# One matmul on nine partitions for the bias table of a decoder layer, spread to 128 rows by its store to DRAM

## What is computed

```python
def t5_bucket(dist):
    n = jnp.maximum(dist, 0)
...
    return jnp.where(n < max_exact, n, large)
...
    def head_bias(bucket):
        nq, nk = bucket.shape
        return rel_bias[bucket].reshape(nq, nk, G, HPG).transpose(2, 3, 0, 1)
...
        s_w = jnp.einsum('bqghd,bkgd->bghqk', qi, kw) * scale + head_bias(t5_bucket(dist))
```

## Time and profile before

| what | us |
|---|---|
| median of three runs | 2054.9 |
| lowest and highest | 2054.63, 2056.81 |
| span of the profiled execution | 2052.7 |
| PE busy in the span | 2019.7 |
| DVE busy | 1393.5 |
| ACT busy | 876.4 |

### The profile page before, as it was taken

The page is one execution under the profiler, slowest core; times in us unless marked ns, Lnnn a source line. Parts: engine busy times, 40 slices in busy tenths (PEclk is TensorE's granted clock), DMA queues, the critical chain, the costliest instruction groups (busy, mean ns, idle before and its releaser), DMA issues.

```text
span 2052.7 us, 26825 instructions
## 1 busy us (share of the span) xinstructions
PE 2019.7 (98%) x9299; PEld 1602.7 (78%) x9299; DVE 1393.5 (68%) x1852; ACT 876.4 (43%) x1127; POOL 36.6 (2%) x56
## 2 busy tenths in 40 slices
PE   7999999999999999999999999999999999999998
PEld 4668888788888888787787878788888888888886
DVE  3557878877778888996556669777774455445454
ACT  4334344344443333543445644544444444434343
POOL 0000000000000000000005000000000000000000
PEclk8999999999999999999999999999999999999999
DMA  9988988899899889798966148599986677676654
GB/s 359 386 314 308 355 318 297 282 299 279 275 320 327 309 308 343 234 367 282 295 195 240 42 147 303 165 281 291 294 249 195 193 206 203 194 217 199 199 185 134
DMA packets 341269, 533.10 MB, mean 260 GB/s; under 512 B 80825, under 2 KB 95252, under 8 KB 340280
## 3 DMA queue, kind: packets, MB, share of 16 engines
q1 hardware_dynamic: 340280, 527.81, 77.8%
q10 hardware_dynamic: 896, 4.06, 0.5%
HBM read 520.04 MB, written 3.89 MB: 255 GB/s over the span
## 4 chain that ended last, share of the span: by engine, by line
PE 94%; DVE 2%; issue 1%; ACT 1%; DMA 1%; ACTq 0%; SPq 0%
PE ps L810 29%; PE ps L812 29%; PE ps L811 29%; PE ps L854 2%; PE ps L839 1%; PE ps L872 1%; DVE ada_acc L1903 1%; PE ps L1333 1%; PE ps L1336 1%; PE ps L1363 1%; DVE w_lo L1885 1%; PE ps L1168 0%; PE ps L1058 0%; ACT w_hi L1457 0%; DMA raw<-in_w_uq_dram 0%
## 5 line engine op out<-in xcount | busy, mean ns | idle before, releaser
L1457 ACT ACTIVATE w_hi<-raw 128x1024 fp32r<-128x1024 f32 (+1 forms) x657 | 689.1, 1054 | 931.5 <-PE ps L812 554.7
L1885 DVE TENSOR_TENSOR w_lo<-raw,w_hi 128x1024 fp32r<-128x1024 f32 (+1 forms) x657 | 796.4, 1220 | 402.4 <-ACT w_hi L1457 398.3
L810 PE MATMUL ps<-w_hi,hT_hi 128*128 128x512 f32 (+1 forms) x1856 | 742.0, 400 | 7.2 <-DVE hT_lo L2020 4.3
L812 PE MATMUL ps<-w_hi,hT_lo 128*128 128x512 f32 (+1 forms) x1856 | 732.1, 394 | 0.0
L811 PE MATMUL ps<-w_lo,hT_hi 128*128 128x512 f32 (+1 forms) x1856 | 732.0, 394 | 0.0
L810 PEld LDWEIGHTS ps<-w_hi,hT_hi 128*128 128x128 f32 x1856 | 350.0, 189 | 102.1 <-issue 14.2
L812 PEld LDWEIGHTS ps<-w_hi,hT_lo 128*128 128x128 f32 x1856 | 350.1, 189 | 83.8
L811 PEld LDWEIGHTS ps<-w_lo,hT_hi 128*128 128x128 f32 x1856 | 350.4, 189 | 80.0 <-issue 0.5
L1903 DVE SCALAR_TENSOR_TENSOR ada_acc<-ada_raw,silu_c,ada_acc 128x512 f32<-128x512 f32 x420 | 315.6, 751 | 8.1
L810 PE MATMUL ps<-w_hi,actT_hi 128*128 128x512 f32 x704 | 280.0, 398 | 0.0
L812 PE MATMUL ps<-w_hi,actT_lo 128*128 128x512 f32 x704 | 279.1, 396 | 0.0
(11 more groups left out here) (235 smaller groups left out, 929.7 us busy)
## 6 DMA issues: line engine op xcount, KB each, us to landing
ada_raw<-in_w_ada_dram SPq DMA_DIRECT2D x224, 512.0 KB, 5.6
raw<-in_w_gate_dram SPq DMA_DIRECT2D x176, 512.0 KB, 4.8
raw<-in_w_up_dram SPq DMA_DIRECT2D x176, 512.0 KB, 5.0
raw<-in_w_down_dram SPq DMA_DIRECT2D x176, 512.0 KB, 4.8
raw<-in_w_in_dram SPq DMA_DIRECT2D x72, 512.0 KB, 5.8
ada_half<-in_w_ada_dram SPq DMA_DIRECT2D x16, 2048.0 KB, 12.7
raw<-in_w_out_dram SPq DMA_DIRECT2D x32, 512.0 KB, 5.0
actT_lo<-norm_tmp SPq DMA_DIRECT2D x240, 32.0 KB, 3.2
```

Source lines behind the costliest of these rows:

```text
L810: pe.matmul(bank, lhs_hi, rhs_hi, start=start, stop=False)
L812: return pe.matmul(bank, lhs_lo, rhs_hi, start=False, stop=stop)
L1457: act.activation(part(U, w_hi, s), part(U, raw, s), ACT.Copy).then_inc(hi_done, 1)
L1885: dve.tensor_tensor(part(U, w_lo, s), part(U, raw, s), part(U, w_hi, s).bitcast(F32), ALU.subtract)\
```

## The change

`rel_rep`, its copy on POOL and eight of the nine matmuls go. One matmul with the nine columns of `rel_sb` gives nine partitions of 384 numbers, one ACT copy takes them to `rev_b` (now 9 x 384), and the store writes every row 128 times: its source repeats each partition's row with a step of zero, its destination is the same DRAM tensor in another order of its dimensions. Two unused tensors keep all other addresses. The waits on `rev_done` shrink to one, ahead of panel 1 of unit 0, because the product sits in PSUM bank 3, which that panel writes.

```diff
-            pool.wait_ge(rel_landed, 16)
-            pool.wait_ge(rel_set, 2)
-            pool.tensor_copy(rel_rep[:, :, :], rel_sb[:, :].unsqueeze(2).broadcast_to([BUCKETS + 1, HEADS + 1, P]))\
-                .then_inc(rel_rep_set, 1)
...
-                if i == 2:
-                    pe.wait_ge(rev_done, HEADS + 1)
...
-                if j < 2 and u == 0:
-                    pe.wait_ge(rev_done, (6, 8)[j])
-                elif j < 2:
+                if (u, j) == (0, 1):
+                    pe.wait_ge(rev_done, 1)
+                elif u == 1 and j < 2:
                     pe.wait_ge(spilled, 2 * j + 2)
...
-            def bias_rows(first, last):
-
-                for h in range(first, last):
-                    if 4 <= h < HEADS:
-                        pe.wait_ge(rev_done, h - 3)
-                    pe.matmul(ps[:, bias_bank(h), 0:384], rel_rep[:, h, :], bucket_sb[:, :], start=True, stop=True)\
-                        .then_inc(rev_mm, 1)
+            def bias_rows():
+
+                pe.wait_ge(rel_set, 2)
+                pe.wait_ge(rel_landed, 16)
+                pe.matmul(ps[0:HEADS + 1, 3, 0:384], rel_sb[:, :], bucket_sb[:, :], start=True, stop=True)\
+                    .then_inc(rev_mm, 1)
...
-            copy_bias_rows(0, 4)
             act.wait_ge(x_landed, 16)
...
-            copy_bias_rows(4, 6)
             copy_rstd("ffn1", T_BANK)
-            copy_bias_rows(6, 8)
             first_hi(0)
             start_hi(0, 1)
-            copy_bias_rows(8, HEADS + 1)
+            act.wait_ge(rev_mm, 1)
+            act.activation(rev_b[:, :], ps[0:HEADS + 1, 3, 0:384], ACT.Copy, scale=1.0 / SCALE).then_inc(rev_done, 1)
...
-            act.wait_ge(rev_done, HEADS + 1)
-            dma(bias_scratch.ap(), rev_b[:, :, :]).then_inc(rev_stored, 16)
+            act.wait_ge(rev_done, 1)
+            dma(bias_scratch.ap().rearrange("p h n -> h p n"), rev_b[:, :].unsqueeze(1).broadcast_to([HEADS + 1, P, 384]))\
+                .then_inc(rev_stored, 16)
```

More of the change, by code:

```diff
@@ L346, in decoder_layer @@
             v_rows = sb("v_rows", [NV, P], within=s)
-            rel_rep = sb("rel_rep", [BUCKETS + 1, HEADS + 1, P], within=s)
+            behind_rel = sb("behind_rel", [P, (HEADS + 1) * P], within=s)
             silu_pad = sb("silu_pad", [P, KD, 32], within=s)
@@ L350, in decoder_layer @@
             behind_half = sb("behind_half", [P, 2240], within=s)
-            rev_b = sb("rev_b", [P, HEADS + 1, 384], within=s)
+            rev_b = sb("rev_b", [HEADS + 1, 384], within=s)
+            behind_rev = sb("behind_rev", [P, HEADS * 384], within=s)
             unshifted = sb("unshifted", [P, 2 * TT, CW], within=s)
@@ L427, in decoder_layer @@
         const_landed, x_landed, rel_landed = sem("const_landed"), sem("x_landed"), sem("rel_landed")
-        rel_set, rel_rep_set = sem("rel_set"), sem("rel_rep_set")
+        rel_set = sem("rel_set")
         ones_set, rows_set = sem("ones_set"), sem("rows_set")
@@ L507, in blocked_before @@
             return u + FF // CW - 1 - BLOCKS_FROM if f == 1 else u - BLOCKS_FROM
-        def bias_bank(h):
-            return T_BANK + 1 if h == HEADS else h % 4
         def ada_use(q, p):
@@ L1046, in first_panel @@
                 pe.wait_ge(nrm["ffn1"]["T_lo_done"], 2 * i + e // 2 + 1)
-                if j < 2 and u == 0:
-                    pe.wait_ge(rev_done, (6, 8)[j])
-                elif j < 2:
+                if (u, j) == (0, 1):
+                    pe.wait_ge(rev_done, 1)
+                elif u == 1 and j < 2:
                     pe.wait_ge(spilled, 2 * j + 2)
                 panel(Unit("gu0", u), j, (hT_hi, hT_lo), j // 2 * 2, 2 * (j % 2), j < 2, j >= KD - 2)
-            def bias_rows(first, last):
-                for h in range(first, last):
-                    if 4 <= h < HEADS:
-                        pe.wait_ge(rev_done, h - 3)
-                    pe.matmul(ps[:, bias_bank(h), 0:384], rel_rep[:, h, :], bucket_sb[:, :], start=True, stop=True)\
-                        .then_inc(rev_mm, 1)
+            def bias_rows():
[3 more added lines that the diff above has]
+                    .then_inc(rev_mm, 1)
             start_half(0)
-            pe.wait_ge(rel_rep_set, 1)
-            bias_rows(0, HEADS + 1)
+            bias_rows()
             start_half(1)
```

## The result

The changed kernel took 2066.06 us in the median of four runs (2065.91 to 2066.94), the kernel before 2055.86 (2054.63 to 2058.49): a ratio of 1.0052, interval 1.0038 to 1.0067. It is slower by 10.2 us, where 2052.5 was forecast and the range ended at 2061.5. The start gave 2.0 of the 2.4 us that were worked out for it. The store, taken at 0, cost 12.3 us.

A forecast was written before the change was run, and what follows sets the result against it. PE was taken as the bound, busy for 98% of the span, with the loads capping the gain. 2054.9 - 2.4 (start) + 0 (store) = 2052.5 us, range 2051.0 to 2061.5.

The forecast's parts named there:

- The start: Up to the first panel: fewer bias products on PE and copies on ACT let `add_start` begin earlier, gaining 2.4 us.
- The store, taken at 0: New store from nine partitions, beside the loads: later loads stay within their spare time, so it costs 0 us.
- rival 2: First two panels: low granted clock or little-moved loads leave a smaller gain, 2053.5 to 2055.4 us; chance 0.19.
- the loads go in step with PE there: Behind the first panel: four panels and two halves take 16.2 us to load, PE's pairs are 16.3 us apart.
- the eighth half: Tightest later load found: lands at 71.9, needed at 74.3; its 2.4 us spare caps the gain at 2.4 to 2.7.
- far bound of 8.1 us: Store's length if each of nine rows has its own engine at 24.3 GB/s; loads come up to 3.5 us later.
- Rival 1: Store's neighbouring rows share a path and delay loads, so PE waits: 2058 to 2068 us; chance 0.24.
- Its m: Factor by which store rows sharing a path last longer; PE waits from 1.9 on, and near 4 was estimated.
- 1.35 + 1.0 m: Time in us of one 512 KB load while the store lasts, each of its 16 rows waiting for one store row.
- that a store which is only slow harms nobody: Store beside the loads: an argument against the rival of rows sharing a path, given without a size.

The follow-up runs named there:

- s_ports: Changed kernel with the nine rows on partitions 0, 12, 24 to 96 instead of 0 to 8; 2052.43 us beside 2056.02 for the kernel before.
- p_two: Changed kernel with the nine rows on partitions 0, 2, 4 to 16, two in each group of four; 2052.37 us beside 2054.64 for the kernel before.
- p_four: Changed kernel, only heads 0 to 3 stored from neighbouring partitions at the old place, five stored earlier from partitions 12 apart; 2065.55 us, ratio 1.0052.
- p_sixteen: Changed kernel with its store issued as nine DMAs, one for each partition's row; 2097.21 us beside 2054.19 for the kernel before, ratio 1.0206.
- p_half: Changed kernel with its store split in two by columns, 2304 rows of 768 B; 2066.1 us beside 2054.64 for the kernel before, ratio 1.0053.
- s_store_only: Kernel before with all its products and copies, only the store replaced by one reading nine partitions 128 times each; 2067.99 us, ratio 1.0061.
- s_split: Changed kernel with its store cut into four of 32 copies, issued ahead of units 2 to 5; 2053.31 us beside 2056.02 for the kernel before.
- s_dram: Changed kernel with the nine rows stored once to DRAM, then copied 128 times by a DRAM to DRAM DMA; 2053.37 us, ratio 0.9991.

## Why the prediction was wrong

**The start: right, term by term, up to the first panel.** The second `start_half` at 21.30 (said: near 21.2), `add_start` at 25.07 (25.0), the first panel at 30.04 (30.1). Behind it the changed kernel went another way than the sum: its first two panels ran at the full granted clock (1.00 from 30 to 36, where the earlier trace rows has 0.50), which rival 2 had priced at 1.7 us, and the first pair of halves came at 35.85, 4.0 us earlier. That the loads go in step with PE there held, but the load that capped the gain was an earlier one than the eighth half: PE stands for an `add_start` that is queued behind a panel's `w_lo`, and that panel landed at 41.2:

```profile
44.22 0.66 PE L832 MATMUL ps<-ident,ada_acc 128*128 128x128 f32 x4 [1.73 <-DVE ada_acc L1896]
```

The second pair of halves is 2.0 us earlier (2.4 said). With a store that costs nothing the forecast of the time comes true: 2052.43 and 2052.37 us in `s_ports` and `p_two`, for 2052.5 predicted. That it is so close is in part luck: beside the kernel before, as it was measured along with them, these are gains of 3.6 and 2.3 us, and the traces have PE 2.0 and 2.3 us ahead near 200 us.

**The store: the step that failed.** "I take **0** for the store" rested on a far bound of 8.1 us, made from nine engines at 24.3 GB/s each. That bound was no bound, for it assumed that nine rows can leave SBUF side by side. The store's packets took 33 us, and PE lost 12.3 us. Nothing in the trace of before shows so narrow a source; an unknown like that needed a wider end, or more weight for the rival.

**Rival 1 was the case, and its mechanism was right in kind.** It had a chance of 0.24. Its m, the number of rows that share a path, is 4: by the rates, partitions 0 to 3 and 4 to 7 each share one path. The Trainium skill, "SBUF — State Buffer", section "Door 1: The DMA port swizzle", puts each four on one port of 27.2 GB/s; the runs bear the grouping out, except for the first 2 us of `p_two`, and have 22.8 to 23.6 GB/s where four rows of a group were read beside loads, which is the figure that counts here. Another of its pages, "DMA: Bandwidth & Descriptors", section "Rules for kernel authors", confines such a store to at most nine engines; queue 10 fits that: 59.7% of 16 engines in `s_ports`, where nine full ones would read 9 / 16 x 1.05 = 59% (full engines read 1.05 in the earlier trace rows), 18.4% in `p_four`, under the 26% of four full ones, and 91.4% in `p_sixteen`. But that rule is not what decided here: nine engines were fast in `s_ports`, and on sixteen the path was as slow.

**Its prices were off.** A load took 4.5 us, not 1.35 + 1.0 m = 5.35; at m = 2 it took 2.2, not 3.35, and PE did not wait, though from m = 1.9 on it should have. The argument against the rival, "that a store which is only slow harms nobody", failed outright: while the slow store ran, the loads of the changed kernel came 4.5 us apart, as if a held-up store packet kept its engine.

**The stand costs more than its length.** The granted clock falls to 0.59 and 0.50 in the stretches behind the two stands, to the low level for some ten products each, and by difference that adds 4.4 us to 7.9. The prediction knew the low clock in the start (rival 2) and forgot it in rival 1's price.

**What stays open:** why the first load behind the store fares worst (14 us, then 4.5 each) and does not in `p_half`, and how `p_two` could run at full rate for 2 us. No run settles either. That a packet of the store blocks its engine is argued from the shares and from `p_half` and `p_four`, not seen on any one engine. That neighbouring partitions share the path, and that the slow store makes the loss, is shown by `s_ports`, `p_two`, `s_store_only` and `p_four`.

## What to carry to other kernels

When a broadcast is moved from an engine into a DMA, look at how many different partitions the DMA reads: here four rows on neighbouring partitions shared one path, and a step of 12 between them cost POOL a small copy and made the same store 2.4 times shorter. A slow store beside the loads of a kernel that lives on loads was not background work: it held up every load while it ran. Cut it into pieces shorter than the spare time of the ring (`s_split`), or take its copies from DRAM (`s_dram`). And of an operation that the trace of before doesn't show, the bound must ask for every shared thing on its way, not only for the engine that issues it.

## What the runs showed of the hardware that was not expected

- A store of 23.4 GB/s from four neighbouring partitions takes the loads from 1.55 to 0.50 MB in 4 us (`p_four`, 256 to 260).
- Halving a row's bytes hardly changed the store's rate (46 GB/s for 47 in 254 to 258) and left the stall as it was (12.2 us for 12.3).
- A queue that is behind holds the engine that issues: 3 to 4.5 us for one load on SP (in the start of the kernel before too, 3.27 us for the panel issued at 42.22), 49.7 us for nine stores on ACT, which then computed nothing.
